# RG-LRU gate matmuls of a streaming encoder: one head on each half of the rows, both gates as columns

## The chip, the cores and the metric

The kernel runs on one core of one Trainium2 chip. Its engines are TensorE (PE in the profile, its weight loads PEld), VectorE (DVE), ScalarE (ACT), GpSimd (POOL) and SyncE (SP), which issues the DMAs. Each engine works through its own instructions in order; semaphores tie them together. The metric is the device time of one execution in microseconds, the median of three.

## The reference, cut to what matters

One step of two layers: layer 0 is a Griffin RG-LRU branch beside sliding-window attention, layer 1 a gated DeltaNet. There are 1024 prompt tokens and 8 x 16 sample tokens, 1152 in all, and everything is float32. The change is in the two gates of the RG-LRU, r and i, which are block diagonal: 8 heads of 64 channels, each with its own 64 x 64 matrices.

```python
def rg_lru(x, h0, w_a, b_a, w_x, b_x, lam):
    xb = xf.reshape(bsz, t, LRU_HEADS, LRU_BLOCK)
    r = sigmoid(einsum('bthi,hij->bthj', xb, w_a).reshape(bsz, t, LRU_WIDTH) + b_a)
    i = sigmoid(einsum('bthi,hij->bthj', xb, w_x).reshape(bsz, t, LRU_WIDTH) + b_x)
    log_a = -LRU_C * r * softplus(-lam)
    a = exp(log_a)
    gated_x = sqrt(-expm1(2.0 * log_a)) * (i * xf)
    # h_t = a_t * h_(t-1) + gated_x_t, along the tokens
```

## The kernel before

Channels lie on the 128 partitions and tokens along the row. The LRU's 512 channels are four groups of 128, m = 0 to 3, each of two heads. The loop tiles(LM, ...) runs over the groups on each engine; the order on each engine is the order in which its function is written, and nothing else sets it.

TensorE, in gates(m): six matmuls of a full 128 x 128 weight tile (the two heads on the diagonal, zeros beside them) against 384 tokens of xc, the convolved input: three thirds of the tokens for gate r, then three for gate i, alternating between PSUM banks 6 and 7. From the third matmul on each waits until the bank's earlier content was read (lz_ev). Then, for m < 3, comes pair(m+1): the input projection of two more 128-column blocks of weights, done by Strassen-like steps 1, 6, 2, 7, 5, 4, 3, each of two parts (four matmuls of 128 x 288). Their results are added up by VectorE (added(p, name), the names u2, c11, u3, c22, u4, c21, c12, line 2535). The steps wait: step 7 for st_cp, ScalarE's copy of step 1's result to P1c (line 1956), which also frees its bank; step 5 for the u2 adds, step 4 for the c11 adds, step 3 for the u3 adds, because these free its banks; step 6 and 3 for sums of the weights by GpSimd (s_made). Behind the last group (m = 3) the remaining projections follow, six tiles of eight matmuls of 128 x 384, and then the attention.

ScalarE, in lru(m): six activations (tanh, line 1994) that read the gates from PSUM into tr (gate r) and ti (gate i); then two over all 1152 tokens (lines 1998 and 1999; the second posts l_a); then copied(m+1), the two copies of line 1956; gate_tanh for the c12 result of the group before; the square root (line 2006) once VectorE posts l_w; then gate_tanh for c11, c22 and c21. The activations that write tr wait for the group before's l_a, those that write ti for the group before's l_y, since the scan's result lies in ti until then.

VectorE, in chain(m), starts at l_a: lines 2600, 2602, 2603, the gates of c12 (line 2593), the u2 adds of the next pair, then line 2610, the scan (line 2612), eight short scans (line 2616), two copies. Behind the chain: the c11 adds, half of the next group's convolution (lines 2571, 2573), the u3 adds, the other half (2577, 2579, 2584, which posts xc_ready), gates and adds in turn, line 2649 (which posts l_y), and the c12 adds.

GpSimd makes four sums of weights for each of pairs 2 and 3 (lines 819 to 827): three when step 7 of the pair before is done, the fourth at that pair's end. SyncE loads the gate weights gw of each group in one DMA when the group before has used them; behind the last group it waits for the c12 gates of group 2 and loads wqkv, which the attention's first matmul needs.

## Time and profile before

| | us |
|---|---|
| median of 3 runs | 1355.46 (1355.41 to 1356.73) |
| the profiled execution's span | 1354.8 |
| TensorE busy | 1325.8 (98%) |
| VectorE busy | 855.6 (63%) |
| ScalarE busy | 434.6 (32%) |
| GpSimd busy | 331.1 (24%) |
| lines 1994, the gates' activations, 24 of 128x384 | 13.9, 581 ns each |

The span runs from the first to the last instruction of one profiled execution. A float32 matmul stands in the trace as two MATMUL records (two passes), and what the notes on the rows call a pass is one of these. A matmul's shape is given by its rows and columns of weights (64*128) and by what it streams (64x256). In a row of the timeline several instructions are merged, x of them; the first number is the start of the first, the second the time from there to the end of the last, and in brackets stands the engine's idle time ahead of them with what ended it.

### The profile page before, as it was taken

The numbers are of one execution on the slowest core, as the hardware profiler recorded it, in microseconds if no ns is written. First come the engines' busy times: TensorE is split into PE (matmuls) and PEld (weight loads), VectorE is DVE, ScalarE is ACT, GpSimd is POOL, SyncE is SP. The second block draws the span as 40 slices with busy tenths as digits, with TensorE's granted clock in tenths as the row PEclk, the third lists the DMA queues.
The fourth block names the chain that finished last, engine by engine and source line by source line (L and its number), as shares of the span: only waits on it lengthen the run. The fifth ranks groups of instructions, "written<-read, shape, count | busy, mean of one in ns | idle before, by whom it ended". The sixth has DMA issues, their size and how long they took to land.

```text
span 1354.8 us, 27409 instructions
## 1 busy us (share of the span) xinstructions
PE 1325.8 (98%) x11200; PEld 904.0 (67%) x11200; DVE 855.6 (63%) x1939; ACT 434.6 (32%) x1044; POOL 331.1 (24%) x450
## 2 busy tenths in 40 slices
PE   5999999999999999999999999999999999999997
PEld 3577776666654454667877788877788777875543
DVE  3847874355454375785886858858578586782246
ACT  3213443344431233521422414224143241432221
POOL 1023200010013232523312423224222242212352
PEclk9999999999999999999999999999999999999999
DMA  9531016002034522121212112121121211440124
GB/s 356 235 75 36 5 36 271 8 1 79 3 130 167 195 85 108 13 81 19 71 46 68 34 34 83 38 77 40 34 83 29 75 50 34 127 159 26 35 94 168
DMA packets 63297, 111.96 MB, mean 83 GB/s; under 512 B 34778, under 2 KB 38690, under 8 KB 61618
## 3 DMA queue, kind: packets, MB, share of 16 engines
q1 hardware_dynamic: 63172, 110.21, 24.2%
q8 instruction: 89, 1.46, 0.4%
q14 instruction: 36, 0.29, 0.1%
HBM read 91.79 MB, written 18.40 MB: 81 GB/s over the span
## 4 chain that ended last, share of the span: by engine, by line
PE 88%; DVE 7%; POOL 1%; DMA 1%; issue 1%; ACT 1%; SPq 0%; DVEq 0%; POOLq 0%; ACTq 0%
PE psum L1132 83%; PE psum L1135 5%; DVE mem L2963 1%; DVE mem L2774 1%; DVE mem L3288 1%; DMA mem<-x_dram 1%; DVE mem L3054 0%; DMA y<-mem 0%; DVE mem L3165 0%; DVE mem L2943 0%; DMA mem<-x 0%; POOL mem L954 0%; DVE mem L2780 0%; ACT mem L1915 0%; ACT mem L2087 0%
## 5 line engine op out<-in xcount | busy, mean ns | idle before, releaser
L1132 PE MATMUL psum<-mem 32*32 32x32 f32 (+12 forms) x10592 | 1264.1, 304 | 4.9 <-DVE mem L2475 1.5
L1132 PEld LDWEIGHTS psum<-mem 128*128 128x128 f32 (+4 forms) x10592 | 835.7, 143 | 401.7 <-issue 217.0
L2963 DVE SCALAR_TENSOR_TENSOR mem<-mem 128x576 f32<-128x576 f32 (+1 forms) x126 | 106.1, 842 | 0.0
L1135 PE MATMUL psum<-mem 128*128 128x128 f32 (+1 forms) x608 | 85.1, 278 | 17.2 <-ACT mem L1927 12.9
L1135 PEld LDWEIGHTS psum<-mem 128*128 128x128 f32 (+1 forms) x608 | 70.7, 144 | 41.4 <-issue 21.0
L2278 ACT ACTIVATE mem<-mem 128x128 f32<-128x128 f32 x72 | 22.0, 305 | 127.6 <-DVE mem L3213 74.4
L2164 ACT ACTIVATE mem<-psum 128x288 f32<-128x288 f32 x28 | 11.4, 407 | 104.0 <-PE psum L1132 104.0
L1011 POOL COPY mem<-mem 128x3 f32<-128x3 f32 x24 | 8.4, 348 | 148.9 <-DVE mem L2921 70.1
L2056 ACT ACTIVATE mem<-mem 128x256 f32<-128x256 f32 x72 | 35.5, 495 | 26.4 <-DVE mem L2697 26.4
L2744 DVE TENSOR_TENSOR mem<-mem,psum 128x512 f32<-128x512 f32 x28 | 19.1, 684 | 37.4 <-PE psum L1132 37.0
L2174 ACT ACTIVATE mem<-mem 128x576 f32<-128x576 f32 (+1 forms) x42 | 32.7, 779 | 28.0 <-DVE mem L2941 28.0
L2682 DVE CUSTOM_DVE_ANT_0 mem<-psum,mem 128x256 f32<-128x256 f32 x72 | 26.2, 419 | 23.4 <-PE psum L1132 23.4
L985 POOL TENSOR_TENSOR mem<-mem 128x512 f32<-128x512 f32 x14 | 15.2, 1088 | 103.8 <-issue 93.3
L2087 ACT ACTIVATE mem<-mem 128x1024 f32<-128x1024 f32 x16 | 16.9, 1056 | 71.5 <-DVE mem L2744 30.3
L2204 ACT ACTIVATE mem<-mem 128x1176 f32<-128x1176 f32 x24 | 28.3, 1178 | 30.2 <-DVE mem L2963 30.2
L2987 DVE SCALAR_TENSOR_TENSOR mem<-mem 128x1024 f32<-128x1024 f32 (+1 forms) x31 | 36.7, 1185 | 0.4 <-ACT mem L2204 0.3
L865 POOL TENSOR_TENSOR mem<-mem 128x512 f32<-128x512 f32 x8 | 9.9, 1268 | 109.9 <-DVE mem L2682 108.7
L1927 ACT ACTIVATE mem<-mem 128x1024 f32<-128x1024 f32 x18 | 20.5, 1144 | 48.6 <-POOL mem L806 26.2
L3174 DVE SCALAR_TENSOR_TENSOR mem<-psum,mem 128x128 f32<-128x128 f32 x56 | 19.4, 346 | 25.4 <-PE psum L1132 25.4
L2774 DVE SCALAR_TENSOR_TENSOR mem<-mem 128x1024 f32<-128x1024 f32 x16 | 20.5, 1281 | 19.7 <-POOL mem L856 14.4
L3190 DVE COPY mem<-psum 128x128 f32<-128x128 f32 x64 | 18.4, 287 | 21.0 <-PE psum L1132 20.9
L3205 DVE SCALAR_TENSOR_TENSOR mem<-mem,psum 128x128 f32<-128x128 f32 x56 | 19.2, 344 | 17.1 <-PE psum L1132 17.1
(260 smaller groups left out, 1277.2 us busy)
## 6 DMA issues: line engine op xcount, KB each, us to landing
mem<-modw SPq DMA_DIRECT2D x12, 2048.0 KB, 12.2
mem<-w SPq DMA_DIRECT2D x44, 512.0 KB, 4.3
mem<-x SPq DMA_DIRECT2D x10, 512.0 KB, 4.7
x_dram<-mem SPq DMA_DIRECT2D x9, 512.0 KB, 2.9
mem<-row_dram SPq DMA_DIRECT2D x8, 576.0 KB, 5.2
mem<-x_dram SPq DMA_DIRECT2D x9, 512.0 KB, 3.7
mem<-wout SPq DMA_DIRECT2D x1, 4096.0 KB, 15.0
mem<-gs SPq DMA_DIRECT2D x8, 512.0 KB, 3.6
```

What stands on the lines that cost most here:

```text
L1132: return pe.matmul(*a, **k)
L1135: return pe.transpose(out, in_, ident[0:n, 0:n])
L1927: act.activation(xh[:, slot], XS[:, t % XSLOTS] if l else X[:, t], ACT.Copy, scale=stat[:, 3 * slot + 2:3 * slot + 3]).then_inc(sem("n_xh" ...
L2056: c.mark(act.activation(SS[:, a], SS[:, a], ACT.Exp, scale=HD ** -0.5, bias=nm[:, a:a + 1], accum_out=den[:, a:a + 1]))
L2174: act.activation(CV[:, m, lo:hi], U1[:, m, lo:hi], ACT.Copy, scale=CW[:, 3 * g + ORDER[m], 0:1]).then_inc(sem("pj_ev"), 1)
L2204: act.activation(U1[:, m, PRE:], CV[:, m, 0:UC], ACT.Tanh, scale=0.5).then_inc(sem("th1"), 1)
L2278: x = act.activation(SQJ, OO[:, k], ACT.Square, accum_out=sso[:, k:k + 1])
L2682: i = dve.tensor_tensor_reduce(SS[:, n], B(bk)[:, a * 256:(a + 1) * 256], mask, 1.0, -3.0e38, ALU.add, ALU.max, mx[:, n:n + 1])
L2774: i = dve.scalar_tensor_tensor(two(tmp), src, rs, two(gate[:, w]), ALU.mult, ALU.mult)
L2963: x = dve.scalar_tensor_tensor(cvm, U1[:, m, lo + j:hi + j], CW[:, 3 * g + ORDER[m], j:j + 1], cvm, ALU.mult, ALU.add)
L2987: dve.scalar_tensor_tensor(S1[:, m, a:b], T[:, a:b], 1.0, CV[:, m, a:b], ALU.add, ALU.mult)
L3174: dve.scalar_tensor_tensor(RR, at_(6, 0), HC[:, 1, k:k + 1], VB[:, k], ALU.mult, ALU.add).then_inc(sem("r_ready"), 1)
```

## The change

A head's 64 input channels now sit on one half of the array's rows, and the 128 columns of its weight tile hold both gates: for the head on rows 0 to 63 gate r in columns 0 to 63 and gate i in 64 to 127, for the head on rows 64 to 127 the other way round. One third of the tokens takes two matmuls of 64 rows, one for each head, into banks 6 and 7. The result of a gate for one head is then on 64 partitions of one bank: for gate r of both heads on the partitions where tr needs it, for gate i on the other half, so ScalarE reads one half and writes the other. It runs twelve activations of 64 partitions, four for a third, where it ran six of 128. The zeros in the weight tile are gone, and gw is loaded by three DMAs.

The thirds also move. third(0) stands where the gates stood; third(1) stands behind step 1 of the pair and third(2) behind step 6 (for m = 3 behind the first and the second projection tile). Each waits until the four activations of the third before have read the banks.

```diff
-        gw = take(2, P)
+        gw = take(2, 64)
...
-                    sp.wait_ge(sem("l_mm"), 6 * m)
-                sp.dma_start(gw, I["gw"][m]).then_inc(sem("gw_in"), 16)
+                    sp.wait_ge(sem("l_mm"), 3 * m)
+                sp.dma_start(gw[0:64], I["gw"][m, 0:64, :, 0:64]).then_inc(sem("gw_in"), 16)
+                for q in range(2):
+                    sp.dma_start(gw[64:, 1 - q], I["gw"][m, 64:, q, 64:]).then_inc(sem("gw_in"), 16)
...
                 for j in range(2):
                     freed(j, 0, "u4")
                     part("1", j, w1, 0, HT, 0, lo(j))
+                if between:
+                    between(1)
...
                     part("6", j, S2, 0, T2, 0, lo(j))
+                if between:
+                    between(2)
...
             def gates(m):
-                pe.wait_ge(sem("gw_in"), 16 * m + 16)
+
+                def third(n):
+
+                    if m or n:
+                        pe.wait_ge(sem("lz_ev"), 12 * m + 4 * n)
+                    for q, r in enumerate((slice(0, 64), slice(64, P))):
+                        i = mm(B(6 + q)[:, 0:NC], gw[r].rearrange("p a c -> p (a c)"), xc[r, n * NC:(n + 1) * NC],
+                               start=True, stop=True)
+                    i.then_inc(sem("l_mm"), 1)
+
+                pe.wait_ge(sem("gw_in"), 48 * m + 48)
...
-                for i in range(6):
-                    if m or i >= 2:
-                        pe.wait_ge(sem("lz_ev"), 6 * m + i - 1)
-                    mm(B(6 + i % 2)[:, 0:NC], gw[:, i // 3], xc[:, (i % 3) * NC:(i % 3 + 1) * NC],
-                       start=True, stop=True).then_inc(sem("l_mm"), 1)
+                third(0)
                 if m < LM - 1:
-                    pair(m + 1)
+                    pair(m + 1, third)
                     return
...
+                        if q == 0 and n:
+                            third(n)
...
-                for i in range(6):
-                    wait(act, sem("l_mm"), 6 * m + i + 1)
-                    if m and i == 0:
-                        wait(act, sem("l_a"), m)
-                    elif m and i == 3:
-                        wait(act, sem("l_y"), m)
-                    dst = (tr, ti)[i // 3][:, (i % 3) * NC:(i % 3 + 1) * NC]
-                    act.activation(dst, B(6 + i % 2)[:, 0:NC], ACT.Tanh, scale=0.5,
-                                   bias=gbias[:, m, i // 3:i // 3 + 1]).then_inc(sem("lz_ev"), 1)
-                wait(act, sem("lz_ev"), 6 * m + 3)
+                top, low = slice(0, 64), slice(64, P)
+                for n in range(3):
+                    wait(act, sem("l_mm"), 3 * m + n + 1)
+                    for i, (dst, r, bank, src) in enumerate(((tr, top, 6, top), (tr, low, 7, low),
+                                                             (ti, top, 6, low), (ti, low, 7, top))):
+                        if m and n == 0:
+                            if i == 0:
+                                wait(act, sem("l_a"), m)
+                            elif i == 2:
+                                wait(act, sem("l_y"), m)
+                        act.activation(dst[r, n * NC:(n + 1) * NC], B(bank)[src, 0:NC], ACT.Tanh, scale=0.5,
+                                       bias=gbias[r, m, i // 2:i // 2 + 1]).then_inc(sem("lz_ev"), 1)
+                wait(act, sem("lz_ev"), 12 * m + 10)
```

The other lines of the change only adapt the counts at which lz_ev and l_mm are awaited.

On TensorE, at the gates of group 0 and the start of pair 1, the rows before stand like this (lz_ev, xc_ready, st_add and so on are the semaphores awaited; 128x384 are gate matmuls, 128x288 those of the pair):

```order
L1132 MATMUL psum<-mem 128x384 [waits mod_done,xc_ready,gw_in]
L1132 MATMUL psum<-mem 128x384
L1132 MATMUL psum<-mem 128x384 [waits lz_ev] x4
L1132 MATMUL psum<-mem 128x288 [waits st_add,w0_in1,w0_in0]
L1132 MATMUL psum<-mem 128x288 x3
L1132 MATMUL psum<-mem 128x288 [waits st_add]
L1132 MATMUL psum<-mem 128x288 x3
L1132 MATMUL psum<-mem 128x288 [waits st_add,t_ready,s_made]
```

and these are the rows of the changed kernel at the same place:

```order
L1134 MATMUL psum<-mem 128x384 [waits mod_done,xc_ready,gw_in]
L1134 MATMUL psum<-mem 128x384
L1134 MATMUL psum<-mem 128x288 [waits st_add,w0_in1,w0_in0]
L1134 MATMUL psum<-mem 128x288 x3
L1134 MATMUL psum<-mem 128x288 [waits st_add]
L1134 MATMUL psum<-mem 128x288 x3
L1134 MATMUL psum<-mem 128x384 [waits lz_ev]
L1134 MATMUL psum<-mem 128x384
L1134 MATMUL psum<-mem 128x288 [waits st_add,t_ready,s_made]
L1134 MATMUL psum<-mem 128x288 x3
L1134 MATMUL psum<-mem 128x288 [waits st_add]
```

Four of the six gate matmuls are gone from the front; two stand behind step 1 (the first two parts of 128x288), and two more, below the rows shown, behind step 6.

On ScalarE, at group 1, the rows before are these (L1994 reads the gates, L1998 and L1999 make a, L1956 is the copy for which step 7 waits):

```order
L1994 ACTIVATE mem<-psum,mem 128x384 [waits l_a,l_mm]
L1994 ACTIVATE mem<-psum,mem 128x384 [waits l_mm] x2
L1994 ACTIVATE mem<-psum,mem 128x384 [waits l_y,l_mm]
L1994 ACTIVATE mem<-psum,mem 128x384 [waits l_mm] x2
L1998 ACTIVATE mem<-mem 128x1152 [waits lz_ev]
L1999 ACTIVATE mem<-mem 128x1152
L1956 ACTIVATE mem<-psum 128x288 [waits g_ev,st_mm] x2
```

and of the changed kernel these, L2015 for L1994, L2019 and L2020 for L1998 and L1999, L1974 for L1956:

```order
L2015 ACTIVATE mem<-psum,mem 64x384 [waits l_a,l_mm]
L2015 ACTIVATE mem<-psum,mem 64x384
L2015 ACTIVATE mem<-psum,mem 64x384 [waits l_y]
L2015 ACTIVATE mem<-psum,mem 64x384
L2015 ACTIVATE mem<-psum,mem 64x384 [waits l_mm]
L2015 ACTIVATE mem<-psum,mem 64x384 x3
L2015 ACTIVATE mem<-psum,mem 64x384 [waits l_mm]
L2015 ACTIVATE mem<-psum,mem 64x384 x3
L2019 ACTIVATE mem<-mem 128x1152 [waits lz_ev]
L2020 ACTIVATE mem<-mem 128x1152
L1974 ACTIVATE mem<-psum 128x288 [waits g_ev,st_mm] x2
```

Twelve of 64 partitions stand where six of 128 stood, the wait for l_y has come from the fourth of six to the third of twelve, and the two over 1152 tokens and the copies stand behind the last third's four.

## Rows read from the trace of the kernel before

**Rows 1.** The page's chain of waits, by engine.
```profile
PE 88%; DVE 7%; POOL 1%; DMA 1%; issue 1%; ACT 1%; SPq 0%; DVEq 0%; POOLq 0%; ACTq 0%
```

**Rows 2.** Stretches: time, busy time (instructions) by engine, granted clock, DMA share, GB/s.
```profile
105.03:109.56 4.53, 4.42 (x14) 2.01 (x13) 0.52 (x2) 2.77 (x5) 3.59 (x7) 1.00 0.69 230
199.97:204.43 4.46, 4.41 (x13) 1.95 (x12) 0.46 (x1) 2.77 (x5) 0.00 (x0) 1.00 0.00 0
109.56:136.72 27.16, 27.16 (x114) 21.28 (x113) 23.20 (x39) 10.04 (x15) 8.18 (x5) 1.00 0.02 6
204.43:235.39 30.96, 30.96 (x98) 18.24 (x96) 13.63 (x23) 10.03 (x14) 0.34 (x2) 1.00 0.69 270
```

**Rows 3.** TensorE's timeline from the second gate pass of group 0.
```profile
105.36 1.13 PE L1132 MATMUL psum<-mem 128*128 128x384 f32 x3
```

**Rows 4.** ScalarE's timeline in group 0.
```profile
105.94 1.17 ACT L1994 ACTIVATE mem<-psum,mem 128x384 f32<-128x384 f32 x2 [17.09 <-PE psum L1132]
...
109.76 0.58 ACT L1994 ACTIVATE mem<-psum,mem 128x384 f32<-128x384 f32 x1
110.23 1.34 ACT L1998 ACTIVATE mem<-mem 128x1152 f32<-128x1152 f32 x1
111.47 1.34 ACT L1999 ACTIVATE mem<-mem 128x1152 f32<-128x1152 f32 x1
112.71 0.39 ACT L1956 ACTIVATE mem<-psum 128x288 f32<-128x288 f32 x1
```

**Rows 5.** VectorE's timeline in group 0: start of the chain, u2 adds, c11 adds.
```profile
112.84 1.36 DVE L2600 TENSOR_TENSOR mem<-mem 128x1152 f32<-128x1152 f32 x1 [7.09 <-ACT mem L1999]
...
116.78 0.45 DVE L2535 TENSOR_TENSOR mem<-mem,psum 128x288 f32<-128x288 f32 x1
117.52 0.45 DVE L2535 TENSOR_TENSOR mem<-mem,psum 128x288 f32<-128x288 f32 x1 [0.29 <-PE psum L1132]
...
122.91 0.81 DVE L2535 TENSOR_TENSOR mem<-mem,psum 128x288 f32<-128x288 f32 x2
```

**Rows 6.** VectorE's timeline: chain and c11 in group 1, c11 and l_y in 2.
```profile
144.47 1.36 DVE L2600 TENSOR_TENSOR mem<-mem 128x1152 f32<-128x1152 f32 x1 [5.72 <-ACT mem L1999]
...
155.02 0.81 DVE L2535 TENSOR_TENSOR mem<-mem,psum 128x288 f32<-128x288 f32 x2
...
186.64 0.81 DVE L2535 TENSOR_TENSOR mem<-mem,psum 128x288 f32<-128x288 f32 x2
...
198.19 1.36 DVE L2649 SCALAR_TENSOR_TENSOR mem<-mem 128x1152 f32<-128x1152 f32 x1
```

**Rows 7.** TensorE's passes and weight loads around the first attention scores.
```profile
249.28 0.59 PE L1132 MATMUL psum<-mem 128*128 128x256 f32 x2
...
249.80 1.60 PEld L1132 LDWEIGHTS psum<-mem 64*128 64x128 f32 x16 [0.33 <-issue]
251.73 0.30 PEld L1132 LDWEIGHTS psum<-mem 128*128 128x128 f32 x2 [0.33 <-issue]
252.27 0.19 PEld L1132 LDWEIGHTS psum<-mem 128*128 128x128 f32 x1 [0.24 <-issue]
```

**Rows 8.** Groups of instructions by shape: busy us, mean ns of one, idle before.
```profile
L2267 ACT ACTIVATE mem<-psum 64x512 f32<-64x512 f32 x8 | 4.7, 592 | 14.1 <-PE psum L1132 14.1
L2065 ACT ACTIVATE mem<-psum 128x512 f32<-128x512 f32 x36 | 19.6, 595 | 29.8 <-PE psum L1135 20.9 <-PE psum L1132 8.9
```

**Rows 9.** GpSimd's second sum and VectorE's line 2579, groups 0 and 2.
```profile
127.21 2.29 POOL L821 TENSOR_TENSOR mem<-mem 128x512 f32<-128x512 f32 x1
...
128.41 2.18 DVE L2579 SCALAR_TENSOR_TENSOR mem<-mem 128x1024 f32<-128x1024 f32 x1
...
191.86 1.28 DVE L2579 SCALAR_TENSOR_TENSOR mem<-mem 128x1024 f32<-128x1024 f32 x1
```

**Rows 10.** The load of wqkv: its issue, and its size and time to landing.
```profile
212.55 0.33 SPq L592 DMA_DIRECT2D mem<-wqkv  x1
mem<-wqkv SPq DMA_DIRECT2D x1, 3072.0 KB, 11.1
```

More of the change, by code:

```diff
@@ L1240, in project, with pair @@
                     i.then_inc(sem(sname), 1)
-            def pair(p):
+            def pair(p, between=None):
                 w1, w2 = PAIR_W[p]
@@ L2565, in conv0 @@
                 if m:
-                    dve.wait_ge(sem("l_mm"), 6 * m)
+                    dve.wait_ge(sem("l_mm"), 3 * m)
                     c.sync()
```

9 lines of the change are left out of this document (5 added, 4 removed).

## Prediction, made before the changed kernel had run

> **What bounds the kernel now.** I read the chain of waits first: TensorE carries 88% of it [rows 1], so a microsecond taken from or put into TensorE's row of work is a microsecond of the span, as long as nothing else arrives late. Then the table of stretches [rows 2]. The gate matmuls of a group take 4.53 us (105.03 to 109.56); the four groups take 4.5, 4.5, 4.5 and 4.5, 17.9 in all. Behind each of the first three stand the 14 parts of the next pair in 27.16 us (112 passes, 1.94 us for a part, 3.88 for the two parts of a step, TensorE busy throughout), and behind the last the projections, 30.96 us. So TensorE repeats every 31.7 us and waits for nobody inside a pair. The question is how far ScalarE's and VectorE's work is from being late. I set T as the start of a group's first gate matmul. In group 0 T is 105.03, and line 1999, the last of ScalarE's work on the gates, ends at 111.47 + 1.34 = 112.81, T+7.8 [rows 4], and with it comes the signal l_a (**a** below) on which VectorE's chain starts; the first c11 add, which frees the bank for TensorE's step 4, starts at 122.91 and takes 0.45, so it is done at T+18.3 [rows 5]. TensorE comes to step 4 at 4.53 + 5 x 3.88 = T+23.9. The slack is 5.6 us. It is not large, and the change spends it.
>
> **A third on TensorE.** A float32 matmul stands in the trace as two passes. 96 passes of 384 columns take 30.96 us [rows 2], 0.323 each; six gate matmuls are 3.9 us and the rest of 4.5 is waiting for evictions. After the change a third is two matmuls of 64 rows. The nearest rows are the attention's scores, 64x128 weights against 256 columns: 16 passes from 249.80 to 251.73, 1.93 us [rows 7]. At 256 columns a pass is 27.16/112 x 256/288 = 0.216, so eight pairs side by side are 1.73 and the switch adds 0.20. Two more bits: the passes of 128 rows behind the run are 252.27 - 251.73 = 0.54 apart where 512 columns take 0.43 (0.11 more), and the last pass ahead of it (the second of two that start at 249.28) would let the next begin at 249.71, it begins at 249.80 (0.09). A third is 2 x 0.323 + 0.20 + 0.11 + 0.09 = 1.05 us; bounds 0.65 (no switching cost) and 1.5 (the two matmuls one after another). Twelve are 12.6 us against 17.9: TensorE alone gains **5.3 us**. By the Trainium skill (TensorEngine Tiling (Array Packing), Overview, Theoretical Speedup) a contraction of 64 or less goes up to twice as fast, an estimate of 0.65 us a third and 0.40 less in each of the twelve, 4.8 us off the sum below; the score rows agree inside the run and add the switching.
>
> **ScalarE.** Six activations of 128x384 become twelve of 64x384. Half the rows are no cheaper: 64x512 takes 592 ns, 128x512 takes 595 [rows 8]. So each keeps its 0.58 us and, back to back, its pitch of 110.23 - 109.76 = 0.48 [rows 4]; a third's four take 3 x 0.48 + 0.58 = 2.0. The Trainium skill (Trainium Kernel Development and Optimization, Best Practices) says that TensorE tiling speeds up compute but not PSUM evacuation; the rows agree, and this is the rule that speaks against the change.
>
> **When the gates are ready.** The rest of the chain stands behind the last third, and that now lies behind steps 1 and 6. Group 0: third 2 begins at 2 x (1.05 + 3.88) = T+9.86. Its first activation starts 0.09 + 0.43 + 0.58 = 1.10 later (the second pass starts 0.43 into the third; 0.58 from a last pass, 105.36, to the activation, 105.94 [rows 3, 4]); four pitches 1.91, line 1998 and 1999 1.24 + 1.34. So a is there at **T+15.4**, 7.6 later than now, while TensorE arrives earlier than now. In this group no third waits for its banks (third 1 comes at T+4.9, they are empty at T+3.2). But P1c's copy (line 1956) is queued on ScalarE behind all twelve activations and the two lines that make a: at 112.71 (T+7.7) now, it then starts at T+15.3 and ends at 15.7. TensorE ends step 2 at 9.86 + 1.05 + 3.88 = 14.8 and must have it for step 7: wait 1.0. Step 7 ends at 19.8. The first u2 add ends 116.78 + 0.45 - 112.81 = 4.4 behind a, T+19.9: wait 0.1. Step 5 ends at 23.9. The first c11 add ends 10.55 behind a, of which 0.29 is a wait for TensorE that goes [rows 5]: T+25.7, wait 1.8. With 0.05 for the release and 0.11 for the exposed weights, steps 4 and 3 (7.76) end at **T+33.6**, and the next group begins.
>
> **VectorE beside GpSimd.** GpSimd's sums start when step 7 ends, now under VectorE's convolution, whose end TensorE needs only at the next group: line 2579 takes 2.18 us beside them and 1.28 alone [rows 9]. After the change they fall before c11, on the path, in groups 0 and 1 (group 2 has none). Bounds 0 and 2.7 (0.9 for each of three sums); no row tells whether the scan, the longest piece of that stretch, is held up at all, so I take 0.5, half a hit of line 2579's kind in each group.
>
> **The sum by groups.** Group 0: 33.6 + 0.5 = 34.1 against 31.7, **+2.4**. Group 1: the activations that write ti wait for l_y of group 0 (line 2649). From c11 to l_y are 198.19 + 1.36 - 187.09 = 12.5 us [rows 6] and from c11 to the next T are 7.9, so l_y comes at T+4.5; two activations later, T+5.7, third 1 may start, TensorE was there at 4.9. Third 2 starts at 5.7 + 0.96 + 3.88 = 10.5, a at 16.1; here a to c11 is 155.02 + 0.45 - 144.44 = 11.0 [rows 6]; + 0.5 + 7.9 = 35.6 against 31.6, **+3.9**. Group 2 the same without GpSimd: 35.1, **+3.4**. Group 3 has no step that waits: its thirds stand between projections, 3 x 1.05 + 30.96 = 34.1 against 35.4, **-1.3**. Sum 2.4 + 3.9 + 3.4 - 1.3 = 8.4, from the unrounded terms **+8.5 us**: the 5.3 us that the matmuls gain are paid back and 13.8 more.
>
> **What hides the rest.** wqkv's load waits for the c12 gates behind a of group 3: it was issued at 212.55, 4.9 behind a (199.97 + 7.7), and takes 11.1 us [rows 2, 10]. After the change a is at T+18.0, the load lands at T+34.0, and TensorE wants it at 34.1: its cover falls from 11.7 us to nothing; 0 to 1 us, taken as 0. The loads behind l_y of group 3 (smask, vc, wout) come up to 20 us later too (9.8 from the groups ahead, 10.3 within this one); their users stand in the attention, behind the 30.96 us of projections and the first queries, and I take that cover as enough. The two more DMAs per group for gw on SP are issued behind third 2, 20 us ahead of use, and hold up nothing: at nothing. Semaphore counts and the halved gw cost nothing.
>
> The span before is 1354.8 us in the profile, 0.7 below the median of 1355.46; the change is added to the median: **1364.0 us**.
>
> **Rivals.** (1) Faster, the chain hidden. If a came so early that steps 7, 5, 4 and ti find their operands, only TensorE's 5.3 us count: 1350.2. For it: 98% busy, and VectorE sits idle 7.09 us ahead of line 2600 [rows 5]. Against it: the slack at step 4 is 5.6, less the 1.4 by which TensorE arrives earlier, 4.2, and a is 7.6 late. It decides at 3.4 us less delay; half-priced activations would give 1.0. Chance 7%. (2) The rows don't run side by side: a third is four passes, 1.5 us, and since each third is on the path to a, twelve cost 0.44 more each: +13.8, 1369.3. The scores speak against it. 5%. (3) GpSimd costs VectorE its full 2.7 in two groups and wqkv comes 1 us late: +8.5 + 4.4 + 1.0, 1369.4. 8%. (4) Partly hidden: no collision, thirds of 0.65 and no wait for l_y (0.8 in two groups): 8.5 - 1.0 - 4.8 - 1.6 = +1.1, 1356.6; 5%. (5) The forecast and its surroundings, 75%.
>
> **Range.** From 8.5, less 1.0 (no collision) and 3.0 (thirds of 0.8, 12 x 0.25), that is 1360.0 (rounded down), up to rivals 2 and 3: **1360.0 to 1369.5**. Outside are rivals 1 and 4 and what is worse than 3. A difference under 0.2% (2.7 us) can't be told from none here: slower 0.88, same 0.05, faster 0.07.
>
> **What would show it.** In the profile after: TensorE waits in a pair for line 1956's successor (step 7, about 1 us) and for VectorE's adds (step 4, about 2 us), in three groups, and for the activations at third 1 in two; starts of groups 34 to 36 us apart; a at T+15 to 16; activations of 64x384 at 0.58; third 1.05. It is wrong if the half-row activations are near 0.3 us, if TensorE shows no waits in a pair, or if its granted clock, 1.00 in every stretch of [rows 2], drops in the new waits.

## The result: 23 us slower, nine beyond the range

The changed kernel takes 1378.85 us (median of 4 runs, 1377.19 to 1379.36) where the kernel before takes 1355.76 on the same chip: a ratio of 1.0169, 95% interval 1.0157 to 1.0182. The direction was forecast, the size was not: 14.9 us above the predicted 1364.0. The page of the changed kernel begins like this:

```profile
span 1376.2 us, 27438 instructions
PE 1327.7 (96%) x11200; PEld 900.8 (65%) x11200; DVE 856.9 (62%) x1939; ACT 448.0 (33%) x1068; POOL 331.2 (24%) x450
```

The program's start takes some 2 us more or less from one execution to the next (last section), so I compare from T of group 0 to the first matmul of the attention's kv: 105.03 to 235.39 before, 130.4 us [rows 2]; 103.07 to 256.35 after, 153.3 us. The 22.9 between them are the whole loss. The same view as [rows 2], of the changed kernel, by group (each stretch runs from a group's T to the next; then the three stretches at half clock; columns as in [rows 2]):

```profile
103.07:142.48 39.41, 33.40 (x125) 23.22 (x124) 23.74 (x39) 16.09 (x25) 12.28 (x11) 0.91 0.08 29
142.48:180.97 38.49, 32.50 (x125) 22.61 (x124) 26.08 (x42) 16.24 (x26) 8.20 (x4) 0.96 0.01 2
180.97:215.87 34.90, 31.06 (x125) 21.68 (x124) 22.94 (x40) 16.60 (x27) 1.27 (x1) 1.00 0.10 33
215.87:256.35 40.48, 36.50 (x109) 20.32 (x109) 18.39 (x34) 17.10 (x27) 0.34 (x2) 0.92 0.24 90
130.15:136.97 6.82, 4.77 (x10) 3.52 (x11) 6.71 (x18) 0.81 (x2) 0.21 (x1) 0.50 0.00 0
171.10:174.50 3.40, 2.88 (x6) 2.17 (x7) 3.36 (x7) 0.81 (x2) 0.00 (x0) 0.50 0.00 0
218.90:225.70 6.80, 4.92 (x8) 2.83 (x9) 2.09 (x3) 1.70 (x3) 0.00 (x0) 0.50 0.00 0
```

Groups of 31.7, 31.6, 31.6 and 35.4 us have become 39.4, 38.5, 34.9 and 40.5. The granted clock, 1.00 in all the four groups before, is 0.50 in three stretches (the lower level, 1.2 GHz; full clock is 2.4). TensorE's timeline shows the waits around them; before, it had none at these places. Line 1974 is ScalarE's copy for step 7, line 2556 VectorE's adds:

```profile
119.22 8.27 PE L1134 MATMUL psum<-mem 128*128 128x288 f32 x32 [1.31 <-ACT mem L1974]
132.20 25.13 PE L1134 MATMUL psum<-mem 128*128 128x288 f32 x92 [4.70 <-DVE mem L2556]
...
163.62 4.15 PE L1134 MATMUL psum<-mem 128*128 128x288 f32 x16 [0.84 <-DVE mem L2556]
171.62 24.20 PE L1134 MATMUL psum<-mem 128*128 128x288 f32 x92 [3.85 <-DVE mem L2556]
...
207.95 8.84 PE L1134 MATMUL psum<-mem 128*128 128x288 f32 x36 [1.69 <-DVE mem L2556]
220.78 39.62 PE L1134 MATMUL psum<-mem 128*128 128x384 f32 x121 [3.98 <-DVE mem L2556]
```

The waits of 4.70 and 3.85 stand before step 4 of groups 0 and 1, the 1.69 before step 4 of group 2, the 3.98 before project 0 of group 3. Half clock begins within each of the three long ones and lasts into the passes behind it; there is none around the 1.69. ScalarE in group 0 (answers [rows 4]):

```profile
108.96 2.38 ACT L2015 ACTIVATE mem<-psum,mem 64x384 f32<-64x384 f32 x4 [2.48 <-PE psum L1134]
113.89 2.38 ACT L2015 ACTIVATE mem<-psum,mem 64x384 f32<-64x384 f32 x4 [2.55 <-PE psum L1134]
116.29 1.35 ACT L2019 ACTIVATE mem<-mem 128x1152 f32<-128x1152 f32 x1
117.55 1.33 ACT L2020 ACTIVATE mem<-mem 128x1152 f32<-128x1152 f32 x1
```

a is posted at 117.55 + 1.33 = 118.88, T+15.8. A third's four activations are 0.60 apart, (2.38 - 0.58) / 3. Thirds 1 and 2 stand 113.89 - 108.96 = 4.93 apart, which is step 6's 3.88 and 1.05 for a third. And VectorE's chain in group 0, which is to be read against [rows 5]:

```profile
118.91 1.36 DVE L2621 TENSOR_TENSOR mem<-mem 128x1152 f32<-128x1152 f32 x1 [15.21 <-ACT mem L2020]
...
123.58 2.45 DVE L2631 SCALAR_TENSOR_TENSOR mem<-mem 128x1152 f32<-128x1152 f32 x1
126.06 3.24 DVE L2633 TENSOR_TENSOR_SCAN mem<-mem 128x1024 f32<-128x1024 f32 x1
129.22 2.20 DVE L2637 TENSOR_TENSOR_SCAN mem<-mem 128x16 f32<-128x16 f32 x8
...
131.60 0.81 DVE L2556 TENSOR_TENSOR mem<-mem,psum 128x288 f32<-128x288 f32 x2
```

GpSimd's timeline at the same time:

```profile
123.55 1.27 POOL L821 TENSOR_TENSOR mem<-mem 128x512 f32<-128x512 f32 x1 [13.92 <-PE psum L1134]
124.89 2.26 POOL L823 TENSOR_TENSOR mem<-mem 128x512 f32<-128x512 f32 x1
127.23 3.12 POOL L825 TENSOR_TENSOR mem<-mem 128x512 f32<-128x512 f32 x1
```

And three pieces of VectorE's chain in group 2, where GpSimd makes no sums:

```profile
202.34 1.35 DVE L2631 SCALAR_TENSOR_TENSOR mem<-mem 128x1152 f32<-128x1152 f32 x1
203.73 2.29 DVE L2633 TENSOR_TENSOR_SCAN mem<-mem 128x1024 f32<-128x1024 f32 x1
205.93 1.25 DVE L2637 TENSOR_TENSOR_SCAN mem<-mem 128x16 f32<-128x16 f32 x8
```

The product, the scan and the small scans take 7.9 us beside GpSimd's sums and 4.9 without them, 3.0 us more on the path (2.1 in group 1).

### The profile page after: what moved, and what is told of

Same layout as the page of the kernel before. It is cut to its first block, busy times and chain, and to the rows that moved or that the text cites. A ratio compares the mean times of both kernels' runs of the same rounds, so it can differ in the third digit from the quotient of the medians.

```text
span 1376.2 us, 27438 instructions
## 1 busy us (share of the span) xinstructions
PE 1327.7 (96%) x11200; PEld 900.8 (65%) x11200; DVE 856.9 (62%) x1939; ACT 448.0 (33%) x1068; POOL 331.2 (24%) x450
## 4 chain that ended last, share of the span: by engine, by line
PE 73%; DVE 6%; POOL 1%; issue 1%; DMA 1%; ACT 1%; DVEq 0%; POOLq 0%; ACTq 0%
PE psum L1134 69%; PE psum L1137 4%; DVE mem L2984 1%; DVE mem L2795 1%; DVE mem L3309 1%; DMA mem<-x_dram 1%; DVE mem L3075 0%; DMA y<-mem 0%; DVE mem L3186 0%; DVE mem L2964 0%; POOL mem L956 0%; DVE mem L2801 0%; ACT mem L2108 0%; DVE mem L3063 0%; DVE mem L3083 0%
## 5 line engine op out<-in xcount | busy, mean ns | idle before, releaser
L1134 PE MATMUL psum<-mem 32*32 32x32 f32 (+13 forms) x10592 | 1265.7, 305 | 25.2 <-DVE mem L2556 15.9
L2077 ACT ACTIVATE mem<-mem 128x256 f32<-128x256 f32 x72 | 35.5, 495 | 26.4 <-DVE mem L2718 26.4
L2015 ACT ACTIVATE mem<-psum,mem 64x384 f32<-64x384 f32 x48 | 27.6, 575 | 46.9 <-PE psum L1134 42.9
L2621 DVE TENSOR_TENSOR mem<-mem 128x1152 f32<-128x1152 f32 x4 | 5.4, 1359 | 58.6 <-ACT mem L2020 58.6
L2225 ACT ACTIVATE mem<-mem 128x1176 f32<-128x1176 f32 x24 | 28.3, 1179 | 30.2 <-DVE mem L2984 30.2
L2795 DVE SCALAR_TENSOR_TENSOR mem<-mem 128x1024 f32<-128x1024 f32 x16 | 20.5, 1281 | 19.7 <-POOL mem L858 14.4
```

The costliest lines, as they stand in the source:

```text
L1134: return pe.matmul(*a, **k)
L2015: act.activation(dst[r, n * NC:(n + 1) * NC], B(bank)[src, 0:NC], ACT.Tanh, scale=0.5, bias=gbias[r, m, i // 2:i // 2 + 1]).then_inc(sem(" ...
L2077: c.mark(act.activation(SS[:, a], SS[:, a], ACT.Exp, scale=HD ** -0.5, bias=nm[:, a:a + 1], accum_out=den[:, a:a + 1]))
L2225: act.activation(U1[:, m, PRE:], CV[:, m, 0:UC], ACT.Tanh, scale=0.5).then_inc(sem("th1"), 1)
L2795: i = dve.scalar_tensor_tensor(two(tmp), src, rs, two(gate[:, w]), ALU.mult, ALU.mult)
```

## The experiments

Sixteen kernels in all, the two of the case among them. The last column is the stretch from T of group 0 to the first kv matmul in the profiled execution. A ratio is to the kernel before on the same chip, with its 95% interval.

| kernel | median us | ratio | T to kv |
|---|---|---|---|
| before | 1355.4 to 1356.2 | 1 | 130.4 |
| changed | 1378.85 | 1.0169 [1.0157, 1.0182] | 153.3 |
| moved | 1376.24 | 1.0147 [1.0130, 1.0164] | 150.8 |
| late_la_6 | 1374.48 | 1.0143 [1.0128, 1.0158] | 149.0 |
| late_la_1 | 1364.38 | 1.0064 [1.0047, 1.0081] | 140.1 |
| paired_front | 1380.15 | 1.0178 [1.0163, 1.0193] | 155.0 |
| front_filled | 1382.02 | 1.0197 [1.0182, 1.0212] | 155.9 |
| front_filled_4 | 1374.41 | 1.0139 [1.0124, 1.0154] | 147.9 |
| filled | 1376.92 | 1.0155 [1.0140, 1.0170] | 152.7 |
| pool_late | 1378.10 | 1.0163 [1.0148, 1.0178] | 153.4 |
| c12_first | 1375.85 | 1.0147 [1.0133, 1.0161] | 150.1 |
| repaired | 1372.92 | 1.0131 [1.0116, 1.0146] | 147.6 |
| repaired_2 | 1372.52 | 1.0125 [1.0108, 1.0142] | 149.1 |
| early_pool_late | 1368.13 | 1.0090 [1.0076, 1.0103] | 141.1 |
| early | 1368.24 | 1.0093 [1.0080, 1.0107] | 142.1 |
| six_front | 1353.96 | 0.9987 [0.9978, 0.9996] | 128.0 |

### Place or form: moved

```diff
+                    for g in range(2):
+                        if m or n:
+                            pe.wait_ge(sem("lz_ev"), 6 * m + 2 * n + g - 1)
+                        mm(B(6 + g)[:, 0:NC], gw[:, g], xc[:, n * NC:(n + 1) * NC],
+                           start=True, stop=True).then_inc(sem("l_mm"), 1)
...
```

> The kernel before with its six full-width gate matmuls (128 rows, 384 columns) and its six 128-row activations kept, but placed where the change places its thirds: two matmuls (one of each gate, same columns) behind the transposes, two behind step 1 of the next pair, two behind its step 6, in the last group inside projection 0. If the time comes from the place of the gates (the state chain starts late, the matmuls of the next steps then wait, and the clock drops in those waits), this kernel is nearly as slow as the changed one: 15 to 20 us above the kernel before (1371 to 1376), la at about T + 15, the step-4 waits of groups 0 and 1 over 3 us, the granted clock at 0.5 behind them. If it comes from the form of the gates (half the rows, columns shared by both gates, activations of 64 rows, results moved across partitions), it stays within 3 us of the kernel before.

1376.24, 20.1 above the kernel before on its chip, where the change is 23.1 above. The gates of the kernel before, full width and evicted by six activations of 128 rows, lose nearly all of it merely by standing where the change puts them. The waits are the same ones too, 4.65 and 4.01 before step 4 and 3.54 before project 0 (line 2548 is VectorE's adds here):

```profile
133.00 30.08 PE L1132 MATMUL psum<-mem 128*128 128x288 f32 x108 [4.65 <-DVE mem L2548]
```

At this place the form of the change is left with the 3 us between the two, and their intervals overlap.

### The late chain alone: late_la_6 and late_la_1

The kernel before with one wait more on ScalarE in groups 0 to 2, ahead of the line that begins a (4 is the end of step 6 of the next pair, 2 the end of step 1). What stands behind that line on ScalarE, the copies for step 7 among it, comes later as well:

```diff
+                if m < LM - 1:
+                    wait(act, sem("st_mm"), STEPS * (m + 1) + 4)
                 wait(act, sem("lz_ev"), 6 * m + 3)
```

> The same with la held back until step 6 of the next pair has ended: la at about T + 12.5, the chain 7.3 us later than before, nearly where the change has it, while matmuls, their columns and the activations stay as they were. Theory: the slack of 5.8 us is overrun by 1.5, GpSimd's sums fall on the chain in groups 0 and 1 for 3 us more, and the clock drops behind these waits for about 2 us each: 6.5 + 6.5 + 1.5 = 14.5, so 1368 to 1373. If so, the late chain alone does what the change does. Rival, the change is slow for its thirds inside the pair, its half-height activations and its reads across partitions, not for the late chain: 1358 at most.

1374.48, above the range of the theory and far from the rival. Not one matmul or activation of the gates was touched. a is posted at T+15.1, and TensorE's waits before step 4 (line 2537 is VectorE's adds here) are like those of the changed kernel:

```profile
133.01 30.57 PE L1132 MATMUL psum<-mem 128*128 128x288 f32 x108 [4.25 <-DVE mem L2537]
...
172.41 13.48 PE L1132 MATMUL psum<-mem 128*128 128x288 f32 x42 [4.48 <-DVE mem L2537]
```

The clock is 0.50 around both, and in group 2 step 4 waits 1.69, as in the changed kernel. From T of group 0 to T of group 3 this kernel takes 111.9 us, the changed one 112.8, the one before 94.9. So in these groups nearly the whole loss comes from when a is posted, and not from the matmuls themselves; in group 3, where nothing is held, this kernel loses 1.6 us (a wait for the gates' activations) and the changed one 5.1.

> The kernel before, with its gates in full, at the front and evicted as they were; only la is held back until step 1 of the next pair has ended, so that it starts at about T + 8.6 instead of T + 5.2 and VectorE's state chain 3.4 us later. Theory (a late la costs only what exceeds the slack): step 4 starts at T + 23.9 and needs c11, which VectorE adds 10.3 us after the chain's start, at T + 18.1 before; 3.4 more are within the slack of 5.8. No waits, no fall of the clock, within 1 us of the kernel before. Rival, every microsecond that the chain starts later is lost: 3.4 in each of three groups, 10 us slower.

1364.38: 9 us slower where none was expected, near the rival's number, though not for the rival's reason. Group 0 behaves as the theory says: TensorE has no wait, the clock is full, and it takes 31.7 us from T to T as before, although a comes 3.4 us later. The slack at step 4 was real. What breaks is the front of the next group. Line 1966 is ScalarE's gate_tanh for c21, which waits for VectorE's adds and stands ahead of the gates' activations (line 1994) in ScalarE's order. TensorE's and then ScalarE's timeline:

```profile
119.78 16.73 PE L1132 MATMUL psum<-mem 128*128 128x288 f32 x67
139.05 23.94 PE L1132 MATMUL psum<-mem 128*128 128x384 f32 x88 [2.54 <-ACT mem L1994]
...
137.72 0.81 ACT L1966 ACTIVATE mem<-mem 128x288 f32<-128x288 f32 x2 [2.29 <-DVE mem L2537]
138.43 1.03 ACT L1994 ACTIVATE mem<-psum,mem 128x384 f32<-128x384 f32 x2
```

and the same place in the timelines of the kernel before, with line 2649, which posts l_y:

```profile
135.68 0.44 ACT L1966 ACTIVATE mem<-mem 128x288 f32<-128x288 f32 x1
137.56 1.23 ACT L1994 ACTIVATE mem<-psum,mem 128x384 f32<-128x384 f32 x2 [1.44 <-PE psum L1132]
139.15 1.23 ACT L1994 ACTIVATE mem<-psum,mem 128x384 f32<-128x384 f32 x2 [0.36 <-PE psum L1132]
...
136.66 1.36 DVE L2649 SCALAR_TENSOR_TENSOR mem<-mem 128x1152 f32<-128x1152 f32 x1
```

ScalarE had 1.44 us to spare between the c21 tanh and the first gate (it waited for TensorE), and the fourth activation, the first to write ti, began at 139.79, 1.8 after l_y was there. Now VectorE's later products come 4.0 us later behind T (3.4 of the hold, the rest GpSimd's), which is 2.6 more than ScalarE had, and TensorE waits 2.54. The same again in group 2, and half clock for 3.4 us behind both waits. The slack on the way into the next group was 1.4 us, not the 5.6 of step 4, and the smaller one decides.

### What the clock costs: filled, paired_front, front_filled, front_filled_4

```diff
+                if p in (1, 2):
+                    pe.wait_ge(sem("lz_ev"), 12 * p)
+                    for k in range((0, 9, 7)[p]):
+                        mm(B(6)[:, 0:SUB], w2[:, 0], HT[:, 0, lo(0)], start=True, stop=True)
                 for j in range(2):
                     pe.wait_ge(sem("st_add"), STEPS * p + ADD["c11"] + j + 1)
```

> The changed kernel with added work whose result is not used: ahead of step 4 of pairs 1 and 2, in TensorE's waits of 5.1 and 4.3 us, 9 and 7 matmuls of 128 rows and 288 columns into a free bank. Theory: the granted clock falls because TensorE stands still in these waits; kept at work it stays at 1.00 behind them, step 4 starts at the same time as in the changed kernel (the wait is VectorE's, not TensorE's), and the 2.2 and 1.2 us that half speed costs in groups 0 and 1 come back: 1375.3, the third drop, in group 3 where nothing is added, stays. Rival, the clock falls for another reason, or the added matmuls cost what they save: 1378 to 1382.

1376.92, 20.7 above before on its chip, so 2.4 less than the changed kernel where 3.5 were expected, and the intervals overlap. The clock did as the theory says. The two stretches in which it was half now show it full; step 4 still waits for VectorE's adds, 0.25 and 0.36 us behind the filling; in group 3, where nothing was added, it drops as before:

```profile
130.00:137.00 7.00, 6.75 (x29) 4.99 (x28) 6.93 (x17) 0.81 (x2) 2.16 (x1) 1.00 0.00 0
171.00:175.00 4.00, 3.64 (x15) 2.58 (x14) 3.93 (x12) 0.81 (x2) 0.00 (x0) 1.00 0.00 0
220.30:227.10 6.80, 5.22 (x8) 2.86 (x9) 1.79 (x3) 1.40 (x3) 0.00 (x0) 0.50 0.00 0
```

T of group 1 comes 37.0 us behind T of group 0 instead of 39.4. But 1.53 of these 2.4 us go at once into a new wait. In the rows of TensorE, ScalarE and VectorE of this kernel, line 2674 posts l_y, 2019 are the activations, and third 1 stands at 148.40:

```profile
148.40 9.92 PE L1134 MATMUL psum<-mem 64*128 64x384 f32 x40 [1.53 <-ACT mem L2019]
...
145.77 1.36 DVE L2674 SCALAR_TENSOR_TENSOR mem<-mem 128x1152 f32<-128x1152 f32 x1
...
147.17 1.18 ACT L2019 ACTIVATE mem<-psum,mem 64x384 f32<-64x384 f32 x2 [0.85 <-DVE mem L2674]
...
159.31 1.36 DVE L2625 TENSOR_TENSOR mem<-mem 128x1152 f32<-128x1152 f32 x1 [11.44 <-ACT mem L2024]
```

These are the links of a **ring**. VectorE works from the chain's start to l_y (120.72 to 147.13, 26.4 us), two activations follow and third 1 may start (1.3), then step 6, third 2, its activations and the two lines of a (10.9), and VectorE's next chain starts at 159.31: 38.6 us round. As long as these pieces take what they take here, no group behind another can be shorter than that, whatever TensorE's clock is. Before the change the ring closed through the front of the group: 25.2 from 112.84 to 138.02, then 4.7 from 139.79 to 144.47, 29.9 in all (30.2 by way of the c21 tanh), under TensorE's 31.6. The change put step 6 and two thirds between l_y and a.

paired_front takes the change's paired matmuls and twelve activations, all three thirds at the front:

```diff
-                third(0)
+                for n in range(3):
+                    third(n)
```

> The changed kernel with its paired matmuls and its twelve activations, but all three thirds ahead of the next pair. A third waits for the four activations of the one before it, so a group's front is two pitches of 3.4 us and the last third's 1.04, 7.8 us instead of the 4.5 of before, and la comes at about T + 12.8. Theory of the place: no matmul of the pair waits over 1 us, no half clock, each of four groups 3.3 us above before: 1368.7 in all, 10 us better than the changed kernel although TensorE now stands idle for the activations. Rival, the form itself costs the time (activations of half height, the moving across partitions, a third's switches between row halves): it stays at 1377 or above.

1380.15, 11.5 us more than expected and no faster than the change (24.0 above before on its chip against 23.1, the intervals overlap). The rival's number came, and part of its reason: at the front the form is dear, since each third waits until the four activations of the one before, 0.60 us apart, have read its banks, so that a is posted at T+14.3 here too. All eight waits for the activations are there, 2.5 to 3.0 each, and each group has half clock around and behind them, 30.6 us in all (the largest and the last of the four stretches):

```profile
107.80:118.00 10.20, 7.04 (x16) 3.81 (x17) 0.00 (x0) 6.49 (x12) 3.60 (x3) 0.50 0.18 67
...
223.90:230.70 6.80, 5.04 (x10) 2.45 (x11) 0.00 (x0) 4.89 (x8) 0.00 (x0) 0.50 0.00 0
```

To price them I filled the waits:

```diff
                 for n in range(3):
+                    if n:
+                        pe.wait_ge(sem("st_add"), STEPS * m + ADD["u4"] + 1)
+                        for k in range(8):
+                            mm(B(pair_bank(m + 1, "1"))[:, 0:SUB], gw.rearrange("p a c -> p (a c)"), xc[:, 0:SUB], ...)
                     third(n)
```

> The kernel with all three paired thirds at the front, whose waits of 2.5 us for the activations pulled the clock to half for 7 to 10 us in every group; in each such wait there are now 8 matmuls of 128 rows and 288 columns into a free bank, their result unused. Theory: the clock stays at 1.00, and what is left is the longer front alone, 3.3 us in each of four groups: 1369, 11 us below the kernel without the added matmuls. Rival, the clock is not moved by the waits, or the paired form costs the rest: 1377 to 1381.

1382.02: an experiment that missed its aim. Each of these matmuls is two passes, so 16 passes filled a wait of 2.5 us and a third's pitch became 4.93 instead of 3.39. The clock did stay full, at equal groups of 38.06 us. With 4 matmuls instead of 8:

> All three paired thirds at the front, with 8 passes of 288 columns in each wait for the activations instead of 16 (16 made a third's pitch 4.93 us, where the activations ask for 3.39). Theory: the pitch falls back to 3.39, what remains of each wait is 0.4 us, and the granted clock stays at 1.00: 8 x 1.54 = 12.3 below the kernel with 16 passes, 1369.7, so that half clock cost the kernel without filling some 10 us. Rival, the clock falls all the same or the passes push the thirds back: 1376 to 1380.

1374.41. Against paired_front this kernel has only more work on TensorE, in waits where it stood idle, and it is 5.7 us faster (5.0 once each is set against before on its chip), intervals apart. That is the cleanest price of the clock here, for 27 us less at half clock. The 19.0 that are left are what the form costs at the front without it, with its waits and its late a. The expected 10 did not come: the waits for the activations shrink to 0.4, but in groups 1 and 2 a wait of 1.77 for l_y stands there, the ring again, and behind the second of them the clock halves for 3.4 us.

### GpSimd and the order on VectorE: pool_late, c12_first

```diff
+                if p >= 2:
+                    wait(pool, sem("st_add"), STEPS * (p - 1) + ADD["c11"] + 2)
```

> The changed kernel with one more wait on GpSimd: its sums of pair p (p = 2, 3) start only when VectorE has added c11 of pair p-1, so that they lie beside nothing of VectorE's state chain. Theory: the chain's product, scan and small scans of groups 0 and 1 fall back from 2.45, 3.24 and 2.20 us to 1.35, 2.29 and 1.25, the waits before step 4 of those groups fall from 5.1 and 4.3 us to about 1.9 and 2.2, and with waits that short the granted clock stays at 1.00 in both; 5.1 us for the chain and 3.4 for the clock, 8.5 in all: about 1370. Rival, the stretched pieces are not GpSimd's doing, or the sums then come too late for pair p and TensorE waits for them: 1377 to 1380.

1378.10, 21.9 above before on its chip, so 1.2 less than the changed kernel, inside the intervals, and no less from T to kv (153.4 against 153.3). That is the rival's number, but not its reason: the theory is right about the cause and wrong about the gain. In VectorE's and then TensorE's timeline the chain's pieces fall back:

```profile
125.03 1.35 DVE L2633 SCALAR_TENSOR_TENSOR mem<-mem 128x1152 f32<-128x1152 f32 x1
126.41 2.29 DVE L2635 TENSOR_TENSOR_SCAN mem<-mem 128x1024 f32<-128x1024 f32 x1
128.62 1.25 DVE L2639 TENSOR_TENSOR_SCAN mem<-mem 128x16 f32<-128x16 f32 x8
...
130.64 8.02 PE L1136 MATMUL psum<-mem 128*128 128x288 f32 x32 [1.69 <-DVE mem L2558]
...
142.05 17.00 PE L1136 MATMUL psum<-mem 128*128 128x288 f32 x56 [2.16 <-DVE mem L2558]
```

The wait at step 4 is 1.69 instead of 4.70 and group 0 takes 34.5 us, near the forecast 34.1. But TensorE is then early at the next place, step 1 of the next pair, which needs VectorE's u4 adds (the row at 142.05), and from within that wait on the clock is half for 6.8 us. The sums still slow VectorE by as much (3.1 us in group 0), now in the convolution and the gates behind it, which lie in the same ring. So this run moves GpSimd's cost rather than taking it out.

```diff
+                if p == PAIRS - 1:
+                    added(p, "c12")
                 gates(m, "c21", U3c)
...
-                added(p, "c12")
+                if p < PAIRS - 1:
+                    added(p, "c12")
```

> The changed kernel with one piece of VectorE's order turned round in the third pass: the additions of c12 of the last pair ahead of its gates c21 and of the multiplication into YT (l_y), not behind them. Theory: project 0 of the last group waits for these additions alone, so it starts 2.4 us earlier (wait 1.6 instead of 4.0 us), and with the shorter wait the granted clock stays at 1.00 behind it or falls for a shorter time: 2.4 to 4.8 us less than the changed kernel, 1374 to 1376.5. Rival, project 0 waits for something else that is as late (l_y, the activations of the third): no change, 1378 to 1379.5.

1375.85, 3.0 us less than the changed kernel, as expected. Project 0 starts 2.65 behind T of group 3 instead of 4.91, and half clock lasts 3.4 us instead of 6.8 (TensorE's timeline, then that stretch):

```profile
218.38 7.09 PE L1134 MATMUL psum<-mem 128*128 128x384 f32 x16 [1.74 <-DVE mem L2556]
...
218.70:222.10 3.40, 3.40 (x7) 1.72 (x6) 1.99 (x3) 1.73 (x3) 0.00 (x0) 0.50 0.00 0
```

This is the one late cost whose repair came through in full; no group follows it.

### All at once: repaired, repaired_2

pool_late and c12_first together, with filling matmuls ahead of step 4 and of third 0 of groups 1 and 2:

```diff
+                    for k in range(5):
+                        mm(B(6)[:, 0:SUB], w2[:, 0], HT[:, 0, lo(0)], start=True, stop=True)
...
+                    for k in range(7):
+                        mm(B(6)[:, 0:SUB], gw.rearrange("p a c -> p (a c)"), xc[:, 0:SUB], start=True, stop=True)
                 third(0)
```

> The changed kernel with every late cost that the runs have shown taken out: GpSimd's sums held until c11 is added, c12 of the last pair added ahead of gates c21 and l_y, and matmuls with an unused result where TensorE waits (5 of 288 columns ahead of step 4, 7 ahead of the first third of groups 1 and 2), so that the clock stays up. Theory: what is left is the late chain itself: step 4 and step 1 of the next pair wait for VectorE, 2.9, 5 and 5 us above before in groups 0 to 2 and next to nothing in group 3: about 1368.5. Rival, these costs hide one another, and taking them out brings others to light: 1373 or more.

1372.92, next to the rival's 1373 and 4.4 above the theory. There is no half clock from the first group to the attention, and 17.5 us of loss are left. 14 passes of filling are more than the wait of 2.2; with 8 there and 6 ahead of step 4:

> The repaired kernel with 8 passes instead of 14 ahead of the first third of groups 1 and 2, and 6 instead of 10 ahead of step 4. Theory: step 1 of the next pair then starts when VectorE has added u4, 21.6 us after its chain began, 1.4 us earlier than before the cut in groups 0 and 1, and group 2 gains the 0.9 of four passes: 3.7 less, 1369 to 1370, with no half clock before the end. What then stands above the kernel before, 14 us, is the late chain alone. Rival, one of the waits left pulls the clock down again, or l_y holds the second third: 1372 or more.

1372.52, from repaired by less than the runs scatter. The rival held: as soon as the filling shrinks, third 1 waits for l_y (1.19 us in groups 1 and 2), and a group cannot be pushed below the ring. VectorE's chains start 37.9 and 38.8 us apart (119.37, 157.28, 196.05). Third 1 of group 1 and the chain's start in the timelines:

```profile
146.37 9.92 PE L1136 MATMUL psum<-mem 64*128 64x384 f32 x40 [1.19 <-ACT mem L2025]
...
157.28 1.36 DVE L2631 TENSOR_TENSOR mem<-mem 128x1152 f32<-128x1152 f32 x1 [11.45 <-ACT mem L2030]
```

One stretch of half clock is back, 3.4 us around the wait of 1.81 before project 0. So with GpSimd's sums off the state chain, the clock held up (fully in repaired) and c12 moved ahead, 17 of the 23 us remain. I put them down to the late chain and its ring, in which GpSimd's sums still lie; no run here takes the sums out altogether.

### Can it be made to pay: early_pool_late, early, six_front

```diff
                 third(0)
+                third(1)
...
-                    between(1)
+                    between(2)
```

(third 1 writes into step 6's two banks, behind VectorE's c21 adds.)

> The change's paired matmuls and twelve activations, with third 1 moved to the front, right behind third 0 (in the two banks that step 6 of the same pair will use, so that it waits for no activation), third 2 behind step 1, and GpSimd's sums of pairs 2 and 3 held until VectorE has added c11 of the pair before. la then comes at about T + 11.6 instead of T + 15.8. Theory (the time is set by how late la comes, since VectorE's work from la to the additions of u4 is what the next pair waits for, and by the waits that pull the clock down): no wait of TensorE over 1 us, the clock at 1.00 throughout, and the front costs 2.7 us instead of 4.5 in each group: 1 to 7 us below the kernel before, 1349 to 1355. Rival, the paired form itself is dear, or la at T + 11.6 is still too late: 1358 or more.

1368.13, the rival. a comes at T+11.6 in group 0 as planned, 10.7 us of the loss are gone, and it is still 12 us slower than before. Third 1 waits 3.89 us at the front of groups 1 and 2, now for the c21 adds that free its banks (line 2571; the row is group 1's):

```profile
138.49 23.20 PE L1142 MATMUL psum<-mem 64*128 64x384 f32 x88 [3.89 <-DVE mem L2571]
```

The chains start 36.0 and 37.5 us apart, and half clock is still there, 3.4 and 6.8 us around these two waits. Moving the third earlier exchanged one late product of VectorE for another.

> The same without the hold on GpSimd: the sums of pairs 2 and 3 start when step 7 of the pair before has ended, about T + 19.3, and lie beside VectorE's scan (T + 20.3 to 22.6) and small scans. Theory: scans of 3.24 instead of 2.29 us and small scans of 2.20 instead of 1.25 in groups 0 and 1, c11 later by 2 to 3 us, waits of 2 to 3 us before step 4 and the clock down behind them: 3 to 7 us above the kernel with the hold. Rival, GpSimd's share is not on the path once la comes earlier: within 1 us of it.

1368.24, the rival: within 0.2 us of the kernel with the hold. GpSimd does stretch VectorE (the small scans take 4.31 us instead of 1.25, c11 waits 2.69), but what it takes before step 4 is given back at third 1, where the wait is 2.03 instead of 3.89.

```diff
-                    if m or i >= 2:
+                    if i in (2, 3):
+                        pe.wait_ge(sem("st_add"), STEPS * m + ADD["c21"] + i - 1)
...
-                    mm(B(6 + i % 2)[:, 0:NC], gw[:, i // 3], ...
+                    mm(B(gate_bank(m, i))[:, 0:NC], gw[:, i // 3], ...
```

> The kernel before with its six full-width gate matmuls at the front as they were, but the third and fourth of them in the two idle banks of step 6, so that none of the first four waits for an activation: a test of what the front costs without the change's pairing. Theory: the front takes 3.9 us instead of 4.5, la comes no later, nothing else moves: 0.6 us less in each of the groups, 1353 to 1354.5 where the kernel before takes 1356. Rival, the front's spare time is given back in the pair's later waits: no difference.

1353.96 (11 runs) against 1355.73 (15 runs), ratio 0.9987 [0.9978, 0.9996], as the theory says: a small gain, but the whole interval lies below 1, and it is faster than both kernels of the case. A group takes 31.04 us from T to T instead of 31.63, TensorE has no wait of over 0.35 us in them, and the clock is full. It is 2.4 us by the traces and 1.8 by the medians, from the gates as they were, with two of them in banks that stood idle. This run has no pairing in it and says nothing for the change.

## Why the prediction was wrong, step by step

It named the right mechanism, a late a for which steps 7, 5 and 4 wait, and the direction follows from it (moved and late_la_6 show it). What failed are three terms of the sum: the granted clock, put at nothing and 6.6 us; group 3, said to have no step that waits, where project 0 waits 4.0; and GpSimd, put at 1.0 us in all and 5.1. TensorE's side holds: the pairs of matmuls run side by side, a third costs 1.05 us as forecast, and rivals 1, 2 and 4 are out; of rival 3 GpSimd's part nearly came, 5.1 of its 5.4. The wait at step 7 was put at 1.0 and is 1.3, that of step 4 without GpSimd at 1.8 and is 1.7 (group 2); the one at step 5, put at 0.1 in group 0, is 0.84 in groups 1 and 2. wqkv held nothing up; no wait for a DMA stands ahead of the kv matmuls. One sentence of the prediction counts wrongly, though its total does not: the matmuls' 5.3 us are set against 13.8 lost, which leaves 8.5, and not 13.8, above before. The missing 14.4 us between T and kv (138.9 forecast, 153.3 measured) lie in these terms, which add up to within 0.2 in each group:

| group | forecast | measured | GpSimd | ScalarE's pitch | l_y | c12 | clock |
|---|---|---|---|---|---|---|---|
| 0 | 34.1 | 39.4 | 2.5 | 0.4 | | | 2.5 |
| 1 | 35.6 | 38.5 | 1.6 | 0.4 | -0.8 | | 1.6 |
| 2 | 35.1 | 34.9 | | 0.4 | -0.8 | | |
| 3 | 34.1 | 40.5 | | | | 4.0 | 2.5 |

- **The clock** (6.6 us) was named as what would make the forecast wrong, and priced at nothing. Steps 4 and 3 take 142.48 - 132.20 = 10.28 us where 7.76 stood in the sum, in group 1 9.35; the projections take 35.57 from 220.78 where 30.96 and two thirds are 33.06. That it falls because TensorE stands idle is shown by filled and front_filled_4, where the same places filled with matmuls keep it at 1.00 (but for 3.4 us in the second).
- **"Group 3 has no step that waits"** is the claim that failed outright. Project 0 needs the banks of the c12 adds. Before, these were ready under the 4.5 us of gates; the change takes that cover down to one third, and VectorE has l_y in front of them. The row at 220.78 is 4.91 behind T instead of 1.05. c12_first shows it: with the adds ahead of l_y 3.0 us are back.
- **GpSimd** (4.1 us) was taken at 0.5 a group, with a bound of 2.7. It is 3.0 in group 0, past the bound, and 2.1 in group 1. No row had told whether the scan would be held up, and I took half a hit for that; it is, by 0.95 (2.29 to 3.24), and so are its two neighbours. The Trainium skill says (Trainium Architecture — The Big Picture, What this means for kernel authors) that only the ports that VectorE and GpSimd share contend, and that this is "an exclusive lock (not a bandwidth split)"; the trace fits that in group 0, whose three hits are 1.10, 0.95 and 0.95 us long whatever the length of the piece, but group 1's first is 0.24, and no run here tests the lock itself.
- **ScalarE's pitch** (0.4 a group) was carried from one shape to another. 0.48 in [rows 4] is the step behind a 128-row activation, and two such that read PSUM follow at 1.03 - 0.57 = 0.46 when both are ready (late_la_1). Those of 64 rows follow at 0.60 throughout the changed kernel. The Trainium skill (ScalarE: Activation LUTs, What ACT_TABLE_LOAD costs) gives an overlap of some 93 ns for activations back to back; the 128-row ones show it (117.55 - 116.29 is 0.09 less than 1.35), the 64-row ones do not. The forecast weighed whether half the rows are cheaper; by the distance from one to the next they are dearer.
- **The wait for l_y** at third 1 was right as a mechanism, at 0.8. It did not appear because T itself came later, and it appears where the groups get shorter (1.53 in filled, 1.77 in front_filled_4, 1.19 in repaired_2).

The table adds up, but its terms are not what a repair brings back. The runs show that they cover one another: moved off the state chain, GpSimd's 4.1 gives 1.2 us; the clock's 4.1 in groups 0 and 1 gives 2.4; and all of it with c12's gives 6.0 of 23.1. A sum that goes through the groups one after another and adds the waits does not show this; the ring does.

Not settled: how much the form itself costs. At the change's place moved leaves it 3.0 us, with overlapping intervals; late_la_6 leaves 4.0, but keeps the six gates' cover ahead of project 0. At the front it costs 19 even with the clock held up (front_filled_4), since its twelve activations hold the two banks. Nor was it tried whether 64-row activations fail to overlap for their height or because each turns to other partitions than the one before.

## What to carry to other kernels

Before work is moved behind other work on the busiest engine, follow its result round until it comes back to itself: buffers that are freed by a late product (here ti through l_y, and the banks through u4 and c21) close rings, and the period is the longest ring, not the busy time of the engine. Take the slack from the tightest of them. Nearly all waits of 2.5 to 4.7 us on TensorE cost more than themselves here, since passes behind them run at half clock; and a late cost is not worth its own length when others stand behind it.

## What was unexpected of the hardware

- Half clock began within or up to 1.4 us behind all waits of 3.5 to 4.7 us and those of 2.5 in late_la_1, ran around those of 2.5 in paired_front, and stood around few of those of 0.8 to 1.8. But the length of the wait alone does not decide it. c12_first's 1.74, repaired_2's 1.81 and front_filled_4's second 1.77 had it and front_filled_4's first 1.77 did not; early's 1.90 before project 0 had it and early_pool_late's 1.90 at the same place did not; and early's 2.69 before step 4 of group 0 did not. In the groups it lasts 3.4, 6.8 or 10.2 us. Passes of 288 columns are then 0.480 us apart instead of 0.2425. Matmuls with an unused result in a wait prevented it.
- Some executions have 3.4 us of half clock at their beginning and some have not. The kernel before has it from 25.9 to 29.3 us, and T of group 0 is 105.03 there; the changed kernel has none, and T is 103.07. In the other traces T is 104.4 to 106.0 with it and 103.0 to 103.5 without, but for repaired, 104.44 without.
- A scan of 16 elements is stretched as much as one of 1024: beside GpSimd's sum one of the eight small scans of group 0 took 1.18 us where the others took 0.22. All eight took 1.25 us alone and 2.20 so; with two of them hit 3.25 (moved), with three 4.31 (early).
